# A head's weighted values placed one projection unit later in a streaming MLA and mLSTM layer

## The reference, cut to what matters

```python
q = (rmsnorm(cq_raw, q_a_norm) @ w_q_up).reshape(B, T, MLA_HEADS, QK_NOPE + QK_ROPE)
q_nope = rmsnorm(q[..., :QK_NOPE], q_nope_norm)
q_pe = rope(rmsnorm(q[..., QK_NOPE:], q_rope_norm), pos)
kv = (ckv @ w_kv_up).reshape(B, S, MLA_HEADS, QK_NOPE + V_HEAD)
k_nope, v = rmsnorm(kv[..., :QK_NOPE], k_nope_norm), kv[..., QK_NOPE:]
s = (einsum('bqhd,bshd->bhqs', q_nope, k_nope) + einsum('bqhd,bsd->bhqs', q_pe, k_pe)) * ATTN_SCALE
p = softmax(where(mask, s, -inf))          # block-causal in chunks of 64 frames
attn = einsum('bhqs,bshd->bqhd', p, v)     # the "weighted values"
```

## Time and profile before

| | us |
|---|---|
| median of 3 runs | 1995.39 (1994.79 to 1996.48) |
| the profiled execution, its own time | 1995.78 |
| its span, first to last instruction | 1994.0 |
| TensorE busy | 1985.5 |
| VectorE busy | 1254.3 |
| ScalarE busy | 911.5 |
| GpSimd busy | 192.7 |
| mean granted TensorE clock | 0.999 of full |

### The profile page before, as it was taken

The page is one execution under the profiler, slowest core; times in us unless marked ns, Lnnn a source line. Parts: engine busy times, 40 slices in busy tenths (PEclk is TensorE's granted clock), DMA queues, the critical chain, the costliest instruction groups (busy, mean ns, idle before and its releaser), DMA issues.

```text
span 1994.0 us, 36219 instructions
## 1 busy us (share of the span) xinstructions
PE 1985.5 (100%) x14762; PEld 1961.7 (98%) x14762; DVE 1254.3 (63%) x2474; ACT 911.5 (46%) x1810; POOL 192.7 (10%) x228
## 2 busy tenths in 40 slices
PE   9999999999999999999999999999999999999998
PEld 9999999999999999999999999999999999999998
DVE  7856677677576786868777555444455664444444
ACT  5564456565444443434444444444444553333333
POOL 0011143433200000000000001000000000000000
PEclk9999999999999999999999999999999999999999
DMA  9765443333455554645545655565556556666665
GB/s 249 197 187 157 113 120 117 99 111 119 122 170 147 149 169 128 179 127 175 157 145 170 169 169 168 168 170 168 173 169 171 169 183 193 193 193 193 193 193 142
DMA packets 219262, 323.24 MB, mean 162 GB/s; under 512 B 28240, under 2 KB 100264, under 8 KB 219096
## 3 DMA queue, kind: packets, MB, share of 16 engines
q1 hardware_dynamic: 215800, 317.71, 55.3%
q10 hardware_dynamic: 3296, 3.22, 0.5%
HBM read 310.06 MB, written 9.62 MB: 160 GB/s over the span
## 4 chain that ended last, share of the span: by engine, by line
PE 99%; DVE 0%; DMA 0%; ACTq 0%; ACT 0%; issue 0%
PE bank L1884 31%; PE bank L1887 30%; PE bank L1888 30%; PE bank L2150 1%; PE bank L2120 1%; PE bank L2046 1%; PE bank L2049 1%; PE bank L2048 1%; PE bank L2222 0%; PE bank L2248 0%; PE bank L2116 0%; PE bank L2117 0%; DMA xt<-in_meta_tokens_dram 0%; PE bank L2260 0%; PE bank L2064 0%; PE bank L2065 0%
## 5 line engine op out<-in xcount | busy, mean ns | idle before, releaser
L1215 DVE TENSOR_TENSOR wlo<-raw,whi 128x512 fp32r<-128x512 f32 (+1 forms) x1256 | 811.0, 655 | 681.5 <-ACT whi L801 671.5
L1884 PE MATMUL bank<-xsplit,whi 128*128 128x288 f32 (+2 forms) x4128 | 1217.2, 295 | 2.4 <-DVE xsplit L1239 2.1
L1888 PE MATMUL bank<-xsplit,wlo 128*128 128x288 f32 (+2 forms) x4128 | 1212.1, 294 | 0.0
L1887 PE MATMUL bank<-xsplit,whi 128*128 128x288 f32 (+2 forms) x4128 | 1211.9, 294 | 0.0
L801 ACT CAST whi<-raw 128x512 fp32r<-128x512 f32 (+1 forms) x1256 | 706.8, 576 | 954.9 <-PE bank L1888 911.6
L1884 PEld LDWEIGHTS bank<-xsplit,whi 128*128 128x128 f32 (+1 forms) x4128 | 773.2, 187 | 5.1 <-issue 3.4
L1887 PEld LDWEIGHTS bank<-xsplit,whi 128*128 128x128 f32 (+1 forms) x4128 | 773.2, 187 | 2.0 <-issue 1.0
L1888 PEld LDWEIGHTS bank<-xsplit,wlo 128*128 128x128 f32 (+1 forms) x4128 | 772.8, 187 | 0.0
L1884 PE MATMUL bank<-latents,whi 128*128 128x288 f32 (+1 forms) x352 | 112.7, 320 | 0.2
L1887 PE MATMUL bank<-latents,whi 128*128 128x288 f32 (+1 forms) x352 | 106.9, 304 | 0.0
L1888 PE MATMUL bank<-latents,wlo 128*128 128x288 f32 (+1 forms) x352 | 106.7, 303 | 0.0
(11 more groups left out here) (301 smaller groups left out, 1254.8 us busy)
## 6 DMA issues: line engine op xcount, KB each, us to landing
raw<-in_w_in_dram SPq DMA_DIRECT2D x313, 512.0 KB, 3.8
raw<-in_w_out_dram SPq DMA_DIRECT2D x128, 512.0 KB, 3.8
raw<-in_w_in_dram SPq DMA_DIRECT2D x142, 256.0 KB, 3.1
raw<-in_w_q_up_dram SPq DMA_DIRECT2D x48, 384.0 KB, 3.3
raw<-in_w_kv_up_dram SPq DMA_DIRECT2D x16, 512.0 KB, 3.7
xres<-in_x_prompt_dram SPq DMA_DIRECT2D x32, 128.0 KB, 3.7
xt<-in_x_prompt_dram SPq DMA_DIRECT2D x28, 128.0 KB, 4.9
out_dram<-ytok SPq DMA_DIRECT2D x28, 128.0 KB, 3.5
```

Source lines behind the costliest of these rows:

```text
L1215: ins = tt(lo, src, hi.bitcast(f32), ALU.subtract)
L1884: ins = mm(out, w_hi, m_hi, start=start, stop=False, **kw)
L1887: mm(out, w_hi, m_lo, start=False, stop=False, **kw)
L1888: return mm(out, w_lo, m_hi, start=False, stop=stop, **kw)
```

## The change

In TensorE's hooks of the attention, the first head's weighted values are issued after unit 12 instead of after unit 11, directly ahead of the transposes of the second head. The queues of the other engines are as before.

```diff
@@ -2161,9 +2161,8 @@
                         scores(phase, i, j, 1)
                     if k == 9:
                         transposes(phase, i, j, 0)
-                    if k == 11:
+                    if k == 12:
                         weighted(phase, i, j, 0)
-                    if k == 12:
                         transposes(phase, i, j, 1)
                     if k == 13:
                         weighted(phase, i, j, 1)
```

## The result

The changed kernel takes 1998.54 us (median of 20 runs, 1997.96 to 2000.46) against 1995.53 us before (20 runs, 1994.52 to 2000.59). The ratio is 1.0015, 95% interval 1.0009 to 1.0021: 3.0 us more, slower by 0.15%. The forecast was 1997.8 us. The profiled execution took 1998.31 us, its span is 1996.5.

A forecast was written before the change was run, and what follows sets the result against it. TensorE, busy nearly throughout, was taken to bound the kernel. Bank 0 waits of +3.07 us less 0.64 us for saved returns gave +2.43 us, so 1995.39 becomes 1997.8 us, 0.12% slower; range 1994.8 to 2000.1 us.

The forecast's parts named there:

- The bound (first part): TensorE, busy 1985.5 of 1994.0 us: changes to its own stream go one for one into the time.
- The cover that goes (b): Unit 12 in seven pairs: without the moved block TensorE waits for VectorE's bank 0 copy, 3.07 us lost.
- d: Time from TensorE's start on unit 12 to the first query copy's start; forecast 0.37 to 0.47 us a pair.
- the rule read from bulk0: From the first projection pair, without attention hooks: loss is d + 0.49 - 0.59 + 0.10, which is d itself.
- Banks 1 and 2: Unit 12's later banks: expected free in time, bank 1 with 0.3 us in hand; stops there bounded the loss at 4.7 us.
- One change of kind less (a): Joined float32 blocks save one return to float32r per pair, 0.08 us each over eight pairs: 0.64 us gained.
- the seam that I could not see: Last weighted matmul followed by first transpose: cost unknown, leaving the gain between 0 and 1.3 us.
- the likeliest case: Bank 0 waits less the saved returns: 1996.6 to 1999.2 us, forecast given 74%.
- ScalarE, GpSimd (c): ScalarE's attnT copy waits for the moved result and transposes need GpSimd's rows; both have over 1.5 us, cost 0.
- Copies in time: Rival: bank 0 is free when TensorE comes, only the 0.64 us gain is left, 1994.8 us; 13%.
- A clock that falls: Rival: every stall halves TensorE's clock for one kv unit, 18.5 us more, 2016 us; 2%.

The follow-up runs named there:

- d = 1.65: Changed kernel with VectorE's three query copies put later, behind the low part of unit 15 in its queue: 2007.11 us, ratio 1.0058 to the kernel before.
- early copies: Changed kernel with VectorE's three query copies put in its hook after unit 10, ahead of the low part of unit 14: 1995.77 us, ratio 0.9998 to before.
- the 1.2 us block: Kernel before with the first head's weighted block inside unit 12, between the matmuls of bank 3 and bank 0, in seven pairs: 1995.90 us, ratio 1.0002.

## Why the prediction was right

**The bound (first part): right.** Everything lost is in TensorE's own stream; the stretches are 3.05 us longer, the medians 3.0. (The spans of the two traces differ by only 2.5 us, because the one after the change reached the first pair 0.5 us sooner: 282.08 against 282.61 us.)

**The cover that goes (b): right in place, mechanism and size.** Forecast 3.07 us, measured 375, 468, 447, 473, 373, 460 and 463 ns (the six matmuls of banks 3 and 0, less 1.182 us), 3.06 us. The loss per pair is d (0.36 to 0.47 us) plus 0.01, nearly the rule read from bulk0, and plus 0.02 at d = 1.65. That the sums agree to 0.01 us is partly luck: in the trace after the change the seven d add up to 3.00 us, not 3.07, and the hundredth that each pair loses beyond its d makes up for it. The copy came when forecast because its path, shown by the chain above, is made of work that the change doesn't move. It was looked for as seven waits of 0.3 to 0.4 us; at the weight load each reads 0.5 to 0.6, because the load normally runs 0.2 ahead (bulk0's own wait, 0.43 us for a d of 0.33, says as much). Banks 1 and 2 did not wait.

**One change of kind less (a): right in kind, mis-sized.** The return did go: the first matmul of unit 12 has a pitch of 0.20 us (316.14 to 316.34) instead of 0.27 to 0.28. But the seam that I could not see costs about half of it. TensorE's timeline after the change, the first transposes behind the block:

```profile
320.41 0.31 PE L2131 MATMUL bank<-con,prob 128*128 128x128 f32 x1
320.56 0.27 PE L2132 MATMUL bank<-con,prob 128*128 128x128 f32 x1
320.67 0.23 PE L2133 MATMUL bank<-con,prob 72*128 72x72 f32 x1
```

The first transpose has a pitch of 0.14 us, the second 0.11. In the eighth pair, where nothing else changes, the stretch is 0.04 us shorter, not 0.08. So the gain is about 8 x 0.045 = 0.36 us (an estimate: the 0.08 less the 0.035 us of the seam), not 0.64.

**A term that was missing.** Unit 12's value matmuls took 1.38 us in all seven pairs before and 1.45 to 1.46 in five after (317.79 to 319.24 above): 0.37 us more in this trace. It eats the rest of (a). The sum becomes 3.06 - 0.36 + 0.37 = 3.07 against the stretches' 3.05. My 2.43 was short by 0.28 at the seam and 0.37 here. The trace before the change shows both times (1.38 us in unit 12, 1.46 us in six pairs of unit 13), but nothing in it says which would come afterwards. That the two missing parts came to no more than 0.65 us together is luck.

**The margins.** By the forecast's own terms (gain between 0 and 1.3 us, d between 0.37 and 0.50) the likeliest case spans 1996.7 to 1998.9 us, not 1996.6 to 1999.2; the measured 1998.54 lies in both. The interval of 1.0009 to 1.0021 tells 3 us apart, which is finer than the 0.2% that the forecast took as the least to be told.

**ScalarE, GpSimd (c): right.** The attnT copy waited (2.36 us idle ahead of it at 320.62) and its place in ScalarE's queue cost nothing that can be seen. No wait appeared at the transposes or the second weighted block.

**The rivals.** Copies in time: refuted by the seven waits; with early copies it comes true, at 1995.77 us where it promised 1994.8, which the interval (0.9989 to 1.0007) still holds. A clock that falls: it stayed at 1.00 through every stall. By the Trainium skill's account of short idles at PSUM banks ("TensorE: Matmul & The Clock Gate", "A second HAM failure mode: psum-queue depth-cycling") it could have dropped; no run here shows it, with one short idle in some 34 us.

## What to carry to other kernels

Where an engine is busy all the time, a block that is "only moved" may be the cover of a copy behind which the next bank opens; read how old that copy is when its bank is wanted, with and without the block. A place in the same kernel where the block is missing, here bulk0, gives the price before anything is built: loss = start of the copy after the start of the unit, plus copy and hand-over, less the work ahead of that bank, plus one slow restart. Two arrangements were free of the stall here: the copy started earlier in its own queue, and other work (the 1.2 us block) directly ahead of the bank.

## What the runs showed of the hardware

- A weight load behind a wait for a semaphore does not run ahead of it (`fill` puts the wait ahead of both load and matmul): after each such wait load and matmul started together, where the load is otherwise some 0.2 us ahead, and the next matmul came 0.30 us later instead of 0.20.
- A return from float32 to float32r matmuls costs 0.08 us (a first pitch of 0.28 us against 0.20); from a float32 matmul to a float32 transpose it is 0.04 (0.143 to 0.147 us against 0.109).
- Twelve 256-column float32r matmuls take 1.38 or 1.46 us, at pitches of 0.11 or 0.12 to 0.13 us in their first eight, at a granted clock of 1.00 in both cases. It varies between executions of one kernel. It isn't explained.
